# Two sequencers of a weight-splitting pipeline: finish the unit two back before splitting the weights two ahead

## The reference

```
def reference(x, ...):
    x = first_block(x, ...)      # per layer: stick-breaking and forgetting attention, then FFN or MoE
    return second_block(x, ...)  # per layer: mLSTM, grouped-query and neighbourhood attention, conv FFN

# first_block, layer l
h = rmsnorm(x, g_mix[l])
p = h @ w_in[l]                                        # queries, keys, values, f, gates
y_sb = merge_heads(stick_breaking_attention(...)) @ w_o_sb[l]
qf, kf = rmsnorm(q_fx, g_q[l]), rmsnorm(k_fx, g_k[l])  # per head
log_f = log_sigmoid(f_pre + b_f[l])
y_fx = merge_heads(forgetting_attention(qf, kf, v, log_f)) @ w_o_fox[l]
g_sb, g_fx = split(sigmoid(gate_pre + b_gate[l]), 2)
x = x + (g_sb * y_sb + g_fx * y_fx) @ w_out[l]
h = rmsnorm(x, g_ffn[l])
x = x + swiglu(h, ...)  or  x + moe_swiglu(h, ...)     # layer 0: dense, layer 1: 8 experts, top 2

# second_block, layer l; xc is a second sequence of 256 tokens, updated in layer 0 only
h, hc = modulate(rms_norm(x), ...), modulate(rms_norm(xc), ...)
parts of h @ w_in[l] and hc @ w_in[l]
y_ml = mlstm_branch(...)      # chunks of 64 tokens in the reference, both directions
y_ga = gqa_latent(...)        # softmax over context and own tokens
y_na = na_latent(...)         # windows of 8 x 16 on a 64-wide grid, and the context
x = x + ga1 * rms_norm(merge_branches(y_ml, y_ga, y_na, zg, ...))
x = x + ga2 * rms_norm(conv_ffn(...))
```

## Time and profile before

| what | value |
|---|---|
| median of 3 runs | 2705.91 us |
| lowest and highest of them | 2704.51 and 2706.21 us |
| profiled execution, its own time | 2701.24 us |
| its span in the trace | 2699.4 us |
| mean granted clock of PE | 0.987 |
| busy: PE, PE's weight loads | 2585.7 us (96%), 2116.9 us (78%) |
| busy: DVE, ACT, POOL | 1740.2 us (64%), 1383.2 us (51%), 103.6 us (4%) |
| read from HBM | 444.63 MB, mean 165 GB/s |

### The profile page before, as it was taken

The page is one execution under the profiler, slowest core; times in us unless marked ns, Lnnn a source line. Parts: engine busy times, 40 slices in busy tenths (PEclk is TensorE's granted clock), DMA queues, the critical chain, the costliest instruction groups (busy, mean ns, idle before and its releaser), DMA issues.

```text
span 2699.4 us, 39835 instructions
## 1 busy us (share of the span) xinstructions
PE 2585.7 (96%) x14356; PEld 2116.9 (78%) x14356; DVE 1740.2 (64%) x2582; ACT 1383.2 (51%) x2241; POOL 103.6 (4%) x112
## 2 busy tenths in 40 slices
PE   8999999998999999999999999999999999998998
PEld 7768898676888888778876777788887678666997
DVE  5755445756998999444455544777774457456776
ACT  5645435654777777434335453542343444545655
POOL 2000001000000000000000100100000010010000
PEclk9999999999999999999999999999999999999999
DMA  7439895445999999332231213467433344334464
GB/s 231 134 125 278 257 315 164 126 133 172 317 329 328 323 316 331 96 71 63 79 91 61 72 59 102 138 182 233 142 120 91 80 124 126 94 107 136 149 188 156
DMA packets 347335, 447.99 MB, mean 166 GB/s; under 512 B 19872, under 2 KB 198176, under 8 KB 347168
## 3 DMA queue, kind: packets, MB, share of 16 engines
q1 hardware_dynamic: 343648, 435.44, 51.3%
q0 software_dynamic: 3232, 9.97, 1.4%
q10 hardware_dynamic: 288, 0.36, 0.0%
HBM read 444.63 MB, written 1.08 MB: 165 GB/s over the span
## 4 chain that ended last, share of the span: by engine, by line
PE 85%; DVE 7%; ACT 4%; issue 3%; POOL 0%; DVEq 0%; POOLq 0%; ACTq 0%
PE ps L2628 21%; PE ps L2615 18%; PE ps L2676 17%; PE ps L2689 8%; PE ps L2680 4%; PE ps L2996 2%; PE ps L3007 2%; PE ps L2697 2%; PE ps L3027 2%; PE ps L2884 2%; PE ps L2715 1%; DVE w_lo L1693 1%; ACT w_hi L1161 1%; PE ps L2989 1%; DVE att L2295 1%
## 5 line engine op out<-in xcount | busy, mean ns | idle before, releaser
L1693 DVE TENSOR_TENSOR w_lo<-raw,w_hi 128x1024 fp32r<-128x1024 f32 (+1 forms) x578 | 687.8, 1201 | 509.3 <-ACT w_hi L1161 449.9
L1161 ACT ACTIVATE w_hi<-raw 128x1024 fp32r<-128x1024 f32 (+1 forms) x578 | 590.0, 1031 | 317.8 <-PE ps L2628 120.1
L2676 PE MATMUL ps<-w_hi,h_hi 128*128 128x512 f32 (+1 forms) x992 | 403.2, 409 | 12.8 <-DVE h_lo L2207 6.5
L2676 PE MATMUL ps<-w_hi,h_lo 128*128 128x512 f32 (+1 forms) x992 | 379.4, 385 | 0.0
L2689 PE MATMUL ps<-w_lo,h_hi 128*128 128x512 f32 (+1 forms) x992 | 297.7, 384 | 0.0
L2615 PE MATMUL ps<-h_hi,w_hi 128*128 128x256 f32 (+1 forms) x1008 | 297.3, 320 | 0.0
L2615 PE MATMUL ps<-h_lo,w_hi 128*128 128x256 f32 (+1 forms) x1008 | 295.7, 318 | 0.0
L2676 PEld LDWEIGHTS ps<-w_hi,h_hi 128*128 128x128 f32 x992 | 187.1, 189 | 71.2 <-issue 31.9
L2689 PEld LDWEIGHTS ps<-w_lo,h_hi 128*128 128x128 f32 x992 | 183.0, 188 | 39.5
L2676 PEld LDWEIGHTS ps<-w_hi,h_lo 128*128 128x128 f32 x992 | 187.2, 189 | 29.4 <-issue 1.0
L2615 PEld LDWEIGHTS ps<-h_hi,w_hi 128*128 128x128 f32 x1008 | 192.0, 190 | 19.7 <-issue 5.8
(11 more groups left out here) (325 smaller groups left out, 4196.7 us busy)
## 6 DMA issues: line engine op xcount, KB each, us to landing
raw<-in_w_in SPq DMA_DIRECT2D x196, 512.0 KB, 3.7
arena<-in_w_mod SPq DMA_DIRECT2D x96, 512.0 KB, 5.1
raw<-in_w_up SPq DMA_DIRECT2D x88, 512.0 KB, 4.0
raw<-in_w_gu_exp SPq DMA_DIRECT2D x64, 512.0 KB, 5.6
arena<-in_w_gu_exp SPq DMA_DIRECT2D x64, 512.0 KB, 4.8
arena<-in_w_gu_exp SPq DMA_DIRECT2D x64, 384.0 KB, 3.9
arena<-in_w_dn_exp SPq DMA_DIRECT2D x48, 512.0 KB, 6.3
raw<-in_w_gu_dense SPq DMA_DIRECT2D x44, 512.0 KB, 8.5
```

The costliest lines, as they stand in the source:

```text
L1161: nc.scalar.activation(w_hi[:, half, 0:n], place[:, 0:n], ACT.Copy).then_inc(seg.sig.hi_ready, 1)
L1693: nc.vector.tensor_tensor(w_lo[:, half, 0:n], place[:, 0:n], w_hi[:, half, 0:n].bitcast(F32), ALU.subtract).then_inc(seg.sig.lo_ready, 1)
L2676: ins = mm(ps[:, 2 * h + p % 2, 0:width], x[:, k + c, p * P:(p + 1) * P], wh[:, c * width:(c + 1) * width], start=opens and c == 0 and x i ...
```

## The change

In the scalar stream and in the vector stream alike, `body` calls `finish_unit(seg, j - AHEAD)` ahead of `split(seg, it, j)` where the segment is paced. In the loop at the end of a segment the same order holds where this segment and the next are both paced; where the next isn't, the split stays ahead of the finish. The other modes, PE's stream, SP's stream and all semaphores stay as they are.

```diff
--- before.py
+++ after.py
@@ -1460,11 +1460,11 @@
 
                 def body(it, before, first):
                     for j in range(seg.n):
+                        if seg.paced and j >= AHEAD:
+                            finish_unit(seg, j - AHEAD)
                         if not first or j >= seg.early:
                             split(seg, it, j)
                         if seg.paced:
-                            if j >= AHEAD:
-                                finish_unit(seg, j - AHEAD)
                             continue
                         if seg.summed is not None and (it, j) in seg.summed.last:
                             act.wait_ge(sum_spread, seg.summed.last[it, j])
@@ -1491,8 +1491,13 @@
                 elif seg.iters == 2:
                     body(1, 0, False)
                 for j in range(AHEAD):
+                    among = seg.paced and seg.next is not None and seg.next.paced
+                    if among:
+                        finish_unit(seg, seg.n + j - AHEAD)
                     if seg.next and not seg.routes:
                         split(seg.next, 0, j)
+                    if among:
+                        continue
                     if seg.paced:
                         finish_unit(seg, seg.n + j - AHEAD)
                     else:
```

## The result

The changed kernel takes 2726.03 us (median of 4 runs, 2725.3 to 2728.25); before, 2705.91. The ratio is 1.0077 with a 95% interval of 1.0059 to 1.0094: 0.8% slower, 20.1 us, and the interval allows 16 to 25. The forecast was 2726. The profiled execution took 2725.59 us, 24.35 more than the profiled execution of before, 2701.24. The work is the same, instruction for instruction in number; it is the waits that differ.

A forecast was written before the change was run, and what follows sets the result against it. PE was taken to bound the kernel, busy 96% of the span. Place terms of 18.3 us plus 1.7 of clock made 20.0, so 2721.2 profiled and 2726 for the median; range 2713 to 2737.

The forecast's parts named there:

- The mechanism: Paced units: weights ready one unit later, so PE waits for w_lo or w_hi behind long finishes; finishes start no sooner.
- mLSTM with its clock: Second block, layer 1, two-tile units: five late w_lo and a smaller one, 7.3 us, plus 1.7 of lower clock.
- head_norm: First block's gate segments, once a layer: w_lo late behind the reduce L2089, 2.3 us each, together 4.6.
- the post-norm: Last mixer: splits late behind ScalarE's squares, root and table load, 2.1 us.
- The step on the decay rows: Later in head_norm's gate segments: PE's 2.04 us wait shifts along with the stall and swallows nothing.
- turn_ctx: Layer 1: VectorE's late split, 0.6 us with the hand-over, then 0.4, 0.2 and 0.1, 1.3 in all.
- The turn into the dense FFN: From mixer into dense FFN: SP's last raw load goes out later, between 0 and 2.4 us, taken as 1.1.
- The clock: Behind the new 3.4 us mLSTM wait PE's granted clock falls, 1.7 us counted once; 6.8 after all four long waits.
- The offset: Runs' median lies 4.67 us above the profiled execution, so 2721.2 there becomes 2725.9 for the median.
- That waits swallow it: Rival: later PE waits absorb the stalls, leaving 5 us, 2711; chance 0.07 together with no effect at all.
- That it adds up: Rival: small margins, late transfers and clock falls after four places add 10.6 us, 2736.6; chance 0.12.
- That steps come sooner: Rival: finishes start sooner and PE's 15.4 us softmax-row waits before L3007 go, 2690.5; chance 0.06.

The follow-up runs named there:

- only_ml: New order on both engines only in the last layer's mLSTM stretch (22 of 769 units), otherwise the kernel before: 2714.85 us, ratio 1.0033.
- the pads: Four runs with two unread VectorE reductions added in 18 mLSTM units: ratios 1.0049 and 1.0041 in the old order, 1.0166 and 1.0164 in the changed kernel.
- dve_only: VectorE alone finishes first, ScalarE keeps the order of the kernel before: 2700.12 us, ratio 0.9983.
- after_pad2: Changed kernel plus two unread VectorE reductions in each of 18 mLSTM units, their output column allocated behind the small tables: 2751.09 us, ratio 1.0164.
- combined_norm: Kernel before, with VectorE alone finishing first in chosen segments, head_norm's included, and attention steps of branch units ahead of saving: 2676.39 us, ratio 0.9889.
- dve_select: Kernel before, with VectorE alone finishing first, except in head_norm's first two gates, last-layer mLSTM and last mixer segments: 2694.02 us, ratio 0.996.
- before_again: The kernel before, unchanged, profiled a second time: 2704.47 us, ratio 1.000.
- before_pad2: Kernel before plus two unread VectorE reductions in each of 18 mLSTM units, their output column allocated behind the small tables: 2717.22 us, ratio 1.0041.
- before_pad: Kernel before plus two unread VectorE reductions in each of 18 mLSTM units, their output column allocated ahead of the raw weight buffers: 2716.69 us, ratio 1.0049.
- steps_first: Kernel before, with the attention steps run ahead of saving the half in VectorE's finish of branch units: 2691.03 us, ratio 0.9952.
- the two pairs: Added VectorE work in old and changed order, run with the output column in two places: 2716.69 and 2747.85 us, then 2717.22 and 2751.09 us.

## Why the prediction was right

**The mechanism, right.** PE waits for w_lo 11.9 us in ten places. Eight are named in the prediction; the other two, 0.30 us each at 122.97 and 560.18, stand directly in front of the waits for the decay rows and are swallowed by them. VectorE's steps keep their distance from PE, L3017's waits stay at 15. only_ml shows that the stretch that carried the largest term costs 9.3 us by itself, and the pads show that it is slack, the unit of distance between split and use, that was spent: work that the old order hides is paid by the new one.

**The terms.** mLSTM with its clock is 9.2 for 9.0, head_norm 4.8 for 4.6, the post-norm 2.3 for 2.1. The step on the decay rows, that they shift along and give nothing back, held for the stalls of 2.4 us: they stand ahead of the evacuation on which the rows hang. It doesn't hold for the stalls of 0.9 us behind that evacuation, at 117 and 547, which the forecast didn't have: 0.76 of each is given back, and this is what took 1.8 us from L2811's wait. dve_only shows that the rows shift along only because VectorE waits for ScalarE's split there. turn_ctx was over-sized by 0.5. The turn into the dense FFN was mis-sized: 2.75 in the trace against 1.1. Its waits, 2.2 us, are within the bound of 2.4; the term lacks the fall of the clock behind them.

**The clock.** I counted 1.7 us once. At the 3.19 us wait the granted clock was 0.54 and then 0.89 in the next two stretches of 3 us, which is 0.46 x 3 + 0.11 x 3 = 1.7 us; the overlaid traces have 1.4 us there, 1.1 net of the wait of 0.38 at L2964 that goes. This wait is followed by a fall in all four traces that have it (3.16 to 3.29 us). At the waits of 2.10, 2.10 and 1.57 us the clock stays up, but it falls behind the new wait of 1.54 us at 228, of which the prediction says nothing. The Trainium skill ("TensorE: Matmul & The Clock Gate", What's actually happening) says that the throttled state is the default and that activity releases it; this trace agrees behind two of these five waits and shows no fall behind the other three. That these three cost nothing is in part luck: the wait near 437 (1.84 to 1.87 us) is followed by a fall in 10 of 14 traces, those of 2.03 and 2.04 us in 4 of 16. The prediction reads the granted clock as a share of time at the upper level; it is a share of full speed, with which its sum of 1.7 is worked out rightly: in after_pad2 it is 0.50 from 2208 to 2214, while PE works. And the trace of before already had waits of 2.04, 2.49 and 2.18 us with no fall behind them, and one of 2.08 at 2113 with one, so the length alone didn't decide.

**The offset.** The sum was 20.0 us, the table's terms that belong to the change 21.1, the medians 20.1. That agreement is better than it deserves: the interval of the measurement reaches from 16 to 25 us, and the turn's 1.6 us too little is partly made up by what turn_ctx and others had too much. For the profiled execution the forecast was 2721.2 and 2725.59 came, as the two profiled executions differ by 24.4, of which some 3.3 is the short first profile. Adding the offset of 4.67 us between profile and median put that right without my knowing why.

**The rivals.** That waits swallow it: three stalls of 0.7 to 0.9 us gave back 0.7 to 0.8 each, none of the large ones did, but for the 0.38 that was forecast. That it adds up: no. That steps come sooner: not in this change (0.5 us at L3017). But the reason that I gave, that a slot is exchanged and not freed, was only half of it: 449.9 us of VectorE's idle time stood in the earlier trace rows, for w_hi, and I read it as harmless because it lies in an engine that isn't the bound. dve_only shows that in 21 places this wait stood in front of something that PE needed. By the Trainium skill ("Perfetto Trace Analysis", Optimization Strategies) the engine that blocks the matmul engine is the one to work on; the gain of combined_norm, 28.9 us, agrees with it.

**Open.** Why work added to VectorE's program slows PE elsewhere (below), what makes the clock fall behind a wait of about 2 us in one execution and not in the next, and part of what dve_select lacks.

## What to carry to other kernels

Where two kinds of work alternate one by one on an engine, swapping them moves no work ahead; it only takes a slot from the distance between producer and consumer, and the price is read off unit by unit as end of the long job plus the short one minus the time of need. If two engines hand work to each other in the same slot, try shifting one of them by a slot, not both: here that took the hand-over out of the chain. And look inside the late job first: two operations that nobody waited for stood in front of the one that PE needed.

## What the runs showed of the hardware that was not expected

The clock that follows a wait of PE is not a property of the kernel alone. Behind the same wait of 1.86 us, and behind the same waits of 2.04 us, the granted clock falls in some executions and stays at 1.00 in others, and a fall there costs 1.0 to 1.7 us. Differences of this size between two traces have to be looked for in the clock before they are put down to a change.

Work added to VectorE's program in one stretch made PE's matmuls slower in others, earlier ones too, with PE's program unchanged. In parts of the FFN loops (from 300, 400 and 1850 us on, above all) the matmuls of 512 columns start every 226 to 227 ns in before_again, and every 230 to 236 ns in before_pad2, at the same granted clock; in other parts both have 226 to 227. The windows of 20 us of the same work, first before_again, then before_pad2:

```profile
...
1890.00:1910.00 20.00, 20.00 (x90) 16.54 (x89) 11.61 (x11) 3.82 (x4) 0.00 (x0) 1.00 0.59 173
...
```

```profile
...
1894.00:1914.00 20.00, 20.00 (x87) 16.14 (x86) 11.13 (x10) 3.82 (x4) 0.00 (x0) 1.00 0.53 158
...
```

90 matmuls in 20 us against 87. Summed over some 5,600 pairs of neighbouring FFN matmuls this is 8.7 us, most of the 12 by which before_pad and before_pad2 are slower; the same sum is under 0.2 us for the changed kernel, dve_only, steps_first and combined_norm, which only reorder instructions. The cause isn't settled: the place of the column is excluded by the two pairs; the length or the place of the added instructions wasn't varied.
